# Two softmax attentions on one core: latent attention's scores two steps ahead with logits and maximum in one instruction, selected attention's meta products on 128 rows

## The chip, the core and the metric

The kernel runs on one core of a Trainium2 chip. Five engines work side by side, each through its own queue in order, and meet at semaphores: TensorE (PE; its weight loads are listed as PEld), VectorE (DVE), ScalarE (ACT), GpSimd (POOL) and SyncE (SP), which here only issues transfers. The metric is the device time of one execution, in microseconds (us). The granted clock of TensorE is given as a share of 2.4 GHz: 1.00 is 2.4 GHz, 0.50 is 1.2 GHz.

## What is computed

The reference runs two blocks of two layers each on 512 tokens of width 1024, in float32. Two attentions matter here. The first layer of block one has a selected attention: 8 heads of 64, 16 meta tokens ahead of the 512, and for each query 128 keys chosen by an index score.

```python
_, idx = lax.top_k(score, topk)
kg = take(k, idx)
vg = take(v, idx)
logits = jnp.einsum('bqhd,bqkhd->bhqk', qb, kg).astype(jnp.float32) * dh ** -0.5
bias = rel_bias[rel_bucket(idx - qpos[None, :, None])]
logits = logits + jnp.transpose(bias, (0, 3, 1, 2)).astype(jnp.float32)
p = jax.nn.softmax(logits, axis=-1).astype(v.dtype)
return jnp.einsum('bhqk,bqkhd->bqhd', p, vg)
```

The first layer of block two has a latent attention: 8 heads of 96 for queries and keys and 64 for values, causal.

```python
sc = jnp.einsum('bqhd,bkhd->bhqk', qb, k,
                preferred_element_type=jnp.float32) * scale
sc = jnp.where(kpos[None, :] <= qpos[:, None], sc, -jnp.inf)
p = jax.nn.softmax(sc, axis=-1)
return jnp.einsum('bhqk,bkhd->bqhd', p.astype(v.dtype), v)
```

Everything else is projections, a gated and a retention linear attention, stick-breaking attention, four gated feed-forward layers, pooling and a convolution.

## The kernel before

Nearly all of TensorE's time goes to dense products (`gemm_k`, lines 486, 490, 493), each made of three float32r products of high and low parts. ScalarE makes the high part of the weights (L459), GpSimd the low part (L466).

Both attentions are one class, `Soft`, with three programs that run side by side: `soft_pe`, `soft_dve`, `soft_act`. Queries are taken in tiles of 128 tokens, t = 1 to 4 (selected attention also has t = 0, the 16 meta tokens). A step is one tile and one head, 8 steps per tile, and tile t sees t key tiles of 128 (selected attention: and the 16 meta keys). A step i is made of:

- `scores(i)` on TensorE (L773) into a bank of PSUM;
- `logits(i)` on VectorE: scale and mask or bias into buffer `lg[i % 2]` (L852), then the negated row maximum (L854). It waits until step i-2 has been transposed out of that buffer;
- `exps(i)` on ScalarE (L910): exponential with row sum. It waits for the maximum of i and for the output of step i-2 (`values_out`, L874), since maxima and sums lie in `mx`, two of each;
- `turn(i)` on TensorE: transposes the probabilities, one product per key tile (L788), and one of the 16 meta columns (L785, selected attention only);
- `turned(i)` on ScalarE copies them to `pt` (L919), and VectorE the 16 meta rows (L863, in `spread`); `spread` also has the reciprocal of the row sum (L865);
- `values(i)` on TensorE (L804): probabilities times values, accumulated over the key tiles. The meta keys come first there, with 16 rows of `pt` and `av`;
- `out(i)` on VectorE: times the reciprocal (L874), into `oa` or `moa`. After a tile's last head `mixed` (L818) transposes its outputs, and a copy or gate and a split into high and low follow (L717, L719, L735, L728).

The order is written out by hand. TensorE per step i: scores(i+1), turn(i), values(i-1), then `fill(i)`, dense k-steps of other layers by a table (latent attention: one in each of the first 16 steps, none later; selected attention: one in each of steps 8 to 31, then every other step). VectorE: logits(i+1), evictions of the dense units (`between`), spread(i), out(i-1). ScalarE: exps(i), turned(i-1). GpSimd adds bias and mask for selected attention (`bm`).

`spare` puts products that nobody reads ahead of the scores: in latent attention six per step from step 17 on (L1351), in selected attention six per step from 6 to 23 and in every other step from 33 on (L2417).

## Time and profile before

| | |
|---|---|
| median of 3 runs | 2734.92 us |
| the three runs | 2734.92, 2715.95, 2737.76 us |
| the profiled execution | 2732.96 us |
| its span on the core | 2731.2 us, mean granted clock 0.975 |
| TensorE busy | 2621.8 us, 96% of the span |
| VectorE, ScalarE, GpSimd busy | 1047.4, 881.9, 1075.9 us |
| share of TensorE in the chain that ended last | 88% |
| selected attention | 284 to 470 us of the span |
| latent attention | 1334 to 1420 us of the span |

Busy time of TensorE counts a product from its start to its modelled end, so neighbours overlap, and a busy TensorE is not TensorE at its peak. Float32 products appear as two records each (the trace's counts x4, x8, x10 are such records for scores and values), transpositions and float32r products as one.

### The profile page before, as it was taken

The numbers are of one execution on the slowest core, as the hardware profiler recorded it, in microseconds if no ns is written. First come the engines' busy times: TensorE is split into PE (matmuls) and PEld (weight loads), VectorE is DVE, ScalarE is ACT, GpSimd is POOL, SyncE is SP. The second block draws the span as 40 slices with busy tenths as digits, with TensorE's granted clock in tenths as the row PEclk, the third lists the DMA queues.
The fourth block names the chain that finished last, engine by engine and source line by source line (L and its number), as shares of the span: only waits on it lengthen the run. The fifth ranks groups of instructions, "written<-read, shape, count | busy, mean of one in ns | idle before, by whom it ended". The sixth has DMA issues, their size and how long they took to land.

```text
span 2731.2 us, 32116 instructions
## 1 busy us (share of the span) xinstructions
PE 2621.8 (96%) x13277; PEld 2146.3 (79%) x13277; DVE 1047.4 (38%) x1740; ACT 881.9 (32%) x1289; POOL 1075.9 (39%) x830
## 2 busy tenths in 40 slices
PE   7999899999998999999889999999999999999999
PEld 6888787887566888877677888878888788888887
DVE  3656343424447322255555222252121444421212
ACT  4433322324654222233534222242222322322221
POOL 3223122431114444444205444445444445444443
PEclk9999987998999999999999999999999999999999
DMA  4222000321013233231103233232233232233222
GB/s 127 63 63 84 27 16 16 109 78 47 16 47 103 94 95 105 89 91 49 55 9 108 94 94 106 85 100 93 93 101 99 88 98 93 93 98 100 96 93 77
DMA packets 215852, 217.78 MB, mean 80 GB/s; under 512 B 10600, under 2 KB 213091, under 8 KB 215707
## 3 DMA queue, kind: packets, MB, share of 16 engines
q1 hardware_dynamic: 215504, 215.68, 24.7%
q8 instruction: 105, 1.72, 0.3%
q14 instruction: 41, 0.33, 0.0%
q10 hardware_dynamic: 202, 0.06, 0.0%
HBM read 213.60 MB, written 2.12 MB: 79 GB/s over the span
## 4 chain that ended last, share of the span: by engine, by line
PE 88%; DVE 5%; ACT 3%; issue 2%; POOL 1%; DMA 1%; ACTq 0%; DVEq 0%; SPq 0%
PE ps L490 65%; PE ps L486 8%; PE ps L493 4%; PE ps L804 2%; PE ps L773 2%; POOL wl L466 1%; ACT wh L459 1%; PE ps L788 1%; PE ps L2417 1%; PE ps L2028 1%; PE ps L1992 1%; PE ps L1475 0%; PE ps L1972 0%; DMA raw<-in_w_in_ab 0%; DVE rstd L567 0%
## 5 line engine op out<-in xcount | busy, mean ns | idle before, releaser
L466 POOL TENSOR_TENSOR wl<-raw,wh 128x512 fp32r<-128x512 f32 x794 | 1047.3, 1350 | 1541.9 <-ACT wh L459 1541.9
L490 PE MATMUL ps<-NH,wh 128*128 128x512 f32 (+1 forms) x1824 | 721.0, 395 | 22.0 <-POOL wl L466 11.3
L490 PE MATMUL ps<-NL,wh 128*128 128x512 f32 (+1 forms) x1824 | 715.8, 392 | 0.0
L490 PE MATMUL ps<-NH,wl 128*128 128x512 f32 (+1 forms) x1824 | 715.0, 392 | 0.0
L459 ACT ACTIVATE wh<-raw 128x2048 fp32r<-128x2048 f32 (+4 forms) x219 | 380.6, 1738 | 479.8 <-PE ps L490 429.3
L490 PEld LDWEIGHTS ps<-NH,wh 128*128 128x128 f32 (+1 forms) x1824 | 345.1, 189 | 104.5 <-POOL wl L466 14.4
L490 PEld LDWEIGHTS ps<-NL,wh 128*128 128x128 f32 (+1 forms) x1824 | 344.7, 189 | 74.8 <-issue 1.7
L490 PEld LDWEIGHTS ps<-NH,wl 128*128 128x128 f32 (+1 forms) x1824 | 344.8, 189 | 73.5
L490 PE MATMUL ps<-GH,wl 128*128 128x512 f32 x832 | 332.8, 400 | 0.0
L490 PE MATMUL ps<-GH,wh 128*128 128x512 f32 x832 | 329.8, 396 | 2.3 <-DVE GL L728 2.3
L490 PE MATMUL ps<-GL,wh 128*128 128x512 f32 x832 | 329.6, 396 | 0.0
L986 DVE SCALAR_TENSOR_TENSOR H<-ps,H 128x512 f32<-128x512 f32 x96 | 66.3, 691 | 341.8 <-PE ps L490 341.8
L490 PEld LDWEIGHTS ps<-GL,wh 128*128 128x128 f32 x832 | 157.2, 189 | 39.8
L490 PEld LDWEIGHTS ps<-GH,wh 128*128 128x128 f32 x832 | 157.3, 189 | 39.2 <-issue 2.6
L490 PEld LDWEIGHTS ps<-GH,wl 128*128 128x128 f32 x832 | 157.0, 189 | 36.4
L953 ACT ACTIVATE GH<-tmp 128x512 fp32r<-128x512 f32 x88 | 55.7, 633 | 374.8 <-DVE tmp L979 374.8
L949 ACT ACTIVATE sg<-sg 128x512 f32<-128x512 f32 x88 | 55.6, 633 | 316.8 <-DVE sg L970 316.8
L970 DVE TENSOR_TENSOR sg<-ps,rstd 128x512 f32<-128x512 f32 x66 | 45.6, 691 | 236.8 <-PE ps L490 236.7
L976 DVE TENSOR_TENSOR tmp<-ps,rstd 128x512 f32<-128x512 f32 x66 | 45.6, 692 | 211.9 <-PE ps L490 211.9
L486 PE MATMUL ps<-NH,wh 128*128 128x264 f32 (+1 forms) x448 | 96.4, 297 | 8.6 <-ACT aqT L1599 4.0
L981 DVE TENSOR_TENSOR GL<-tmp,GH 128x512 fp32r<-128x512 f32 x88 | 73.3, 833 | 61.5 <-ACT GH L953 61.5
L493 PE MATMUL ps<-wh,NH 128*128 128x256 f32 (+1 forms) x320 | 91.5, 286 | 2.1 <-ACT bv L1606 2.1
(390 smaller groups left out, 3099.9 us busy)
## 6 DMA issues: line engine op xcount, KB each, us to landing
raw<-in_ffn_w_gate SPq DMA_DIRECT2D x44, 1024.0 KB, 5.4
raw<-in_ffn_w_up SPq DMA_DIRECT2D x44, 1024.0 KB, 5.3
raw<-in_ffn_w_down SPq DMA_DIRECT2D x32, 1024.0 KB, 4.9
raw<-in_w_in_ab SPq DMA_DIRECT2D x16, 1024.0 KB, 5.5
raw<-in_w_in_cd SPq DMA_DIRECT2D x14, 1024.0 KB, 5.0
raw<-in_ffn_w_down SPq DMA_DIRECT2D x16, 768.0 KB, 4.2
raw<-in_c_w_in SPq DMA_DIRECT2D x12, 1024.0 KB, 5.1
raw<-in_w_out_ab SPq DMA_DIRECT2D x8, 512.0 KB, 3.4
```

Of the source, the lines that this page charges most:

```text
L459: nc.scalar.activation(wh[:, b % 2, 0:k, 0:w], raw[:, b % 2, 0:k, 0:w], ACT.Copy).then_inc(S("weights_high"), 1)
L466: ins = nc.gpsimd.tensor_tensor(wl[:, b % 2, ks, 0:w], raw[:, b % 2, ks, 0:w], wh[:, b % 2, ks, 0:w].bitcast(F32), ALU.subtract)
L486: last = nc.tensor.matmul(ps[0:m1 - m0, bank + h, 0:T // 2], w[:, s, k, m0:m1], x(k)[:, h * (T // 2):(h + 1) * (T // 2)], start=start, sto ...
L490: last = nc.tensor.matmul(ps[0:m1 - m0, bank, 0:SEQ], w[:, s, k, m0:m1], x(k), start=start, stop=stop)
L493: last = nc.tensor.matmul(ps[0:n_tok, bank, 0:total], x(k)[:, c0:c0 + n_tok], w[:, s, k, 0:total], start=start, stop=stop)
L773: last = nc.tensor.matmul(ps[0:n, A.score_at[i % len(A.score_at)] + x, 0:w], A.q(h, c0, n), A.k(h, x * w, w), start=True, stop=True)
L804: last = nc.tensor.matmul(ps[0:n, A.value_at[i % len(A.value_at)], 256:256 + HD], A.pt[0:kn, i % 2, a0:a0 + n], A.v(kt, h), start=(x == 0) ...
L949: nc.scalar.activation(sg[:, i, :], sg[:, i, :], ACT.Silu).then_inc(S("gate_silu"), 1)
L953: nc.scalar.activation(GH[:, 2 * p_ + i, :], tmp[:, i, 0:SEQ], ACT.Copy).then_inc(S("hidden_high"), 1)
L970: nc.vector.tensor_tensor(sg[:, i, :], ps[:, bank_of(u + i), :], r, ALU.mult).then_inc(S("evac_dve"), 1)
L981: nc.vector.tensor_tensor(GL[:, 2 * p_ + i, :], tmp[:, i, 0:SEQ], GH[:, 2 * p_ + i, :].bitcast(F32), ALU.subtract).then_inc(S("hidden_low" ...
L986: nc.vector.scalar_tensor_tensor(out=H[:, m, META:T], in0=ps[:, bank_of(u), :], scalar=0.5, in1=H[:, m, META:T], op0=ALU.mult, op1=ALU.add ...
```

## The change

Latent attention (`mla`) gets `ahead=2` and `negated=True`:

- scores(0) and scores(1) are issued first; then per step TensorE runs turn(i), scores(i+2), values(i-1), fill(i), and VectorE between(i), spread(i), logits(i+2), out(i-1);
- logits and row minimum come from one VectorE instruction, `tensor_tensor_reduce`: (scores + mask) times the negated `qroot`, minimum accumulated. The exponential takes them with scale -1. One more instruction negates `qroot` beforehand;
- its spare products are gone.

Both attentions: `mx` has four sums in place of two, and exps(i) waits for the output of step i-4 in place of i-2.

Selected attention (`dsa`) keeps its order and its spare products. The meta product of `values` takes all 128 rows of `pt` and `av` instead of 16; rows 16 to 127 are cleared once (`av` before the selection rounds, `pt` before the attention).

```diff
@@ soft_pe
             for x, kt in enumerate(kts):
-                kn = META if kt == 0 else P
                 a0 = 4 * P if kt == 0 else (kt - 1) * P
-                last = nc.tensor.matmul(ps[0:n, A.value_at[i % len(A.value_at)], 256:256 + HD], A.pt[0:kn, i % 2, a0:a0 + n], A.v(kt, h),
+                last = nc.tensor.matmul(ps[0:n, A.value_at[i % len(A.value_at)], 256:256 + HD], A.pt[:, i % 2, a0:a0 + n], A.v(kt, h),
                                         start=(x == 0), stop=(x == len(kts) - 1))
...
-        scores(0)
+        for i in range(A.ahead):
+            scores(i)
         for i in range(N):
-            if i + 1 < N:
+            if A.ahead == 1 and i + 1 < N:
                 scores(i + 1)
             turn(i)
+            if A.ahead == 2 and i + 2 < N:
+                scores(i + 2)
             if i >= 1:
                 values(i - 1)
@@ soft_dve
+            if A.negated:
+                nc.vector.tensor_tensor_reduce(out=A.lg[0:n, i % 2, 0:w], in0=ps[0:n, s0, 0:w], in1=b, scale=A.scale(t, n, h), scalar=BIG,
+                                               op0=ALU.add, op1=ALU.min, accum_out=A.mx[0:n, i % 2, :]).then_inc(S(tg + "_logits"), 1)
+                return
...
-            step(dve, nc.vector.reciprocal(A.mx[0:n, 2 + i % 2, :], A.mx[0:n, 2 + i % 2, :]))
+            step(dve, nc.vector.reciprocal(A.mx[0:n, 2 + i % 4, :], A.mx[0:n, 2 + i % 4, :]))
...
             spread(i)
+            if A.ahead == 2 and i + 2 < N:
+                logits(i + 2)
             if i >= 1:
                 out(i - 1)
@@ soft_act
-            act.wait_ge(S(tg + "_max"), i + 1)
-            if i >= 2:
-                act.wait_ge(S(tg + "_values_out"), i - 1)
+            act.wait_ge(S(tg + ("_logits" if A.negated else "_max")), i + 1)
+            if i >= 4:
+                act.wait_ge(S(tg + "_values_out"), i - 3)
             w = A.width(t)
-            nc.scalar.activation(A.lg[0:n, i % 2, 0:w], A.lg[0:n, i % 2, 0:w], ACT.Exp, bias=A.mx[0:n, i % 2, :],
-                                 accum_out=A.mx[0:n, 2 + i % 2, :]).then_inc(S(tg + "_exp"), 1)
+            nc.scalar.activation(A.lg[0:n, i % 2, 0:w], A.lg[0:n, i % 2, 0:w], ACT.Exp, bias=A.mx[0:n, i % 2, :], scale=-1.0 if A.negated else 1.0,
+                                 accum_out=A.mx[0:n, 2 + i % 4, :]).then_inc(S(tg + "_exp"), 1)
@@ second_dve
         step(dve, nc.vector.reciprocal(qroot[:, :, :], qroot[:, :, :]))
+        step(dve, nc.vector.tensor_scalar(qroot[:, :, :], qroot[:, :, :], -1.0, None, ALU.mult))
@@ second_pe
-        def mla_spare(i):
-
-            for x in range(MLA_SPARE[i]):
-                nc.tensor.matmul(ps[:, mla.score_at[i % 2], 0:SEQ // 2], GH[:, x % 4, 0:P], GH[:, (x + 1) % 4, 0:SEQ // 2], start=True, stop=True)
-        mla.spare = mla_spare
@@ dsa
-               lambda kt, h: av[0:token_tile(kt)[1], kt, h * HD:(h + 1) * HD],
+               lambda kt, h: av[:, kt, h * HD:(h + 1) * HD],
@@ vector program
         index_dve(dve)
+        nc.vector.memset(av[:, 0, :], 0.0).then_inc(S("av_zero"), 1)
...
+        step(dve, nc.vector.memset(pt[:, :, 4 * P:5 * P], 0.0))
         soft_dve(dve, dsa, lambda e: e.wait_ge(S("strip_out"), HEADS))
```

ScalarE waits for `av_zero` before it writes the first tile of `av`.

TensorE's queue in latent attention at t = 3, in its order. L773 or L775 are scores, L788 or L790 transpositions, L804 or L805 values, L1351 the spare products. Before:

```order
L773 MATMUL ps<-ktT,qtT 128x384
L788 MATMUL ps<-K_53,mlg 128x128 x3
L804 MATMUL ps<-kvtok,mpt 128x64 x3
L1351 MATMUL ps<-GH 128x256 x6
L773 MATMUL ps<-ktT,qtT 128x384
L788 MATMUL ps<-K_53,mlg 128x128 x3
```

and after:

```order
L790 MATMUL ps<-K_53,mlg 128x128 x3
L775 MATMUL ps<-ktT,qtT 128x384
L805 MATMUL ps<-kvtok,mpt 128x64 x3
L790 MATMUL ps<-K_53,mlg 128x128 x3
L775 MATMUL ps<-ktT,qtT 128x384
```

The scores moved from ahead of the transpositions to behind them and belong to a step one later; the six products are gone.

VectorE's queue at the same tile, with a tile's closing copy (L717 or L718) in it: `mlg` are the logits, `mmx` maxima and sums, `moa` the outputs. Before:

```order
L852 SCALAR_TENSOR_TENSOR mlg<-ps,qroot,K_133 128x384
L854 TENSOR_REDUCE mmx<-mlg 128x1
L717 COPY tmp<-ps 128x512
L865 RECIPROCAL mmx<-mmx 128x1
L874 TENSOR_SCALAR moa<-ps,mmx 128x64
```

and after:

```order
L873 RECIPROCAL mmx<-mmx 128x1
L853 ISA mlg,mmx<-ps,K_133,qroot 128x384
L853 ISA mmx 128x1
L882 TENSOR_SCALAR moa<-ps,mmx 128x64
L718 COPY tmp<-ps 128x512
```

The logits of the step after next stand behind the reciprocal and ahead of the output. The one instruction of the source is two rows, the second of which writes one column.

## Rows read from the trace of the kernel before

**Rows 1.** The page, 40 slices of the span, tenths of TensorE's full clock.

```profile
PEclk9999987998999999999999999999999999999999
```

**Rows 2.** Busy time of each engine in four stretches (us from the span's start).

```profile
core 0: us, PE busy (x) PEld busy (x) DVE busy (x) ACT busy (x) POOL busy (x), PEclk, DMA share, GB/s
351.00:380.00 29.00, 28.05 (x195) 23.70 (x194) 14.50 (x45) 8.55 (x26) 9.16 (x10) 1.00 0.06 19
380.00:433.40 53.40, 52.91 (x204) 42.63 (x204) 18.83 (x49) 11.51 (x29) 12.53 (x11) 0.55 0.04 11
1334.00:1367.00 33.00, 27.65 (x146) 20.84 (x147) 20.26 (x66) 14.84 (x51) 4.16 (x4) 1.00 0.11 33
1367.00:1412.40 45.40, 42.82 (x286) 33.48 (x286) 28.30 (x66) 19.63 (x49) 2.51 (x2) 1.00 0.04 12
```

**Rows 3.** Waits in latent attention: engine, line, releaser: total us, times, longest.

```profile
ACT mlg L910 <- DVE moa L874: 39.0, 27, 1.9
PEld ps L788 <- ACT mlg L910: 21.5, 29, 1.7
```

**Rows 4.** Timeline of latent attention, one step at t = 4 (start, duration, instruction).

```profile
1397.54 0.72 ACT L910 ACTIVATE mlg<-mlg,mmx 128x512 f32<-128x512 f32 x1 [1.81 <-DVE moa L874]
...
1397.88 1.02 PE L773 MATMUL ps<-ktT,qtT 96*128 96x512 f32 x2
1398.16 0.19 ACT L910 ACTIVATION_READ_ACCUMULATOR mlg<-mlg,mmx 128x1 f32 x1
...
1398.74 0.60 PE L788 MATMUL ps<-K,mlg 128*128 128x128 f32 x4
...
1399.18 1.00 PE L804 MATMUL ps<-kvtok,mpt 128*128 128x64 f32 x8
...
1399.99 0.96 PE L1351 MATMUL ps<-GH 128*128 128x256 f32 x6
```

**Rows 5.** Waits of TensorE in selected attention, 323 to 470 us.

```profile
PEld ps L804 <- issue: 7.1, 33, 0.6
...
PE ps L486 <- DVE H L1412: 3.3, 6, 1.0
...
PE ps L785 <- ACT lg L910: 1.9, 3, 1.1
```

**Rows 6.** Timeline of TensorE in latent attention, t = 2 and t = 3.

```profile
1359.89 0.44 PE L788 MATMUL ps<-K,mlg 128*128 128x128 f32 x2
...
1361.42 0.59 PE L773 MATMUL ps<-ktT,qtT 96*128 96x256 f32 x2
...
1381.74 0.55 PE L788 MATMUL ps<-K,mlg 128*128 128x128 f32 x3
...
1382.80 0.96 PE L1351 MATMUL ps<-GH 128*128 128x256 f32 x6
```

**Rows 7.** Timeline of VectorE, ahead of latent attention and at t = 4.

```profile
1316.15 0.34 DVE L1246 RECIPROCAL qroot<-qroot 128x32 f32<-128x32 f32 x1
...
1395.58 0.75 DVE L852 SCALAR_TENSOR_TENSOR mlg<-ps,qroot,K 128x512 f32<-128x512 f32 x1 [1.25 <-PE ps L773]
1396.37 0.69 DVE L854 TENSOR_REDUCE mmx<-mlg 128x1 f32<-128x512 f32 x1
```

**Rows 8.** Timeline of TensorE in selected attention, a step at t = 4.

```profile
437.81 0.60 PE L788 MATMUL ps<-K,lg 128*128 128x128 f32 x4
438.34 1.47 PE L804 MATMUL ps<-av,pt 16*128 16x64 f32 x10
```

**Rows 9.** Busy time and granted clock in stretches of 3 us.

```profile
382.00:385.00 3.00, 2.52 (x15) 1.85 (x15) 1.95 (x5) 0.88 (x3) 1.03 (x1) 1.00 0.00 0
385.00:388.00 3.00, 2.99 (x10) 2.41 (x10) 0.40 (x3) 1.10 (x3) 0.00 (x0) 0.52 0.00 0
```

**Rows 10.** Timeline of TensorE before and at the end of the slow stretch.

```profile
382.03 0.94 PE L773 MATMUL ps<-akT,aqT 64*128 64x200 f32 x4
...
385.01 0.67 PE L486 MATMUL ps<-MH,wh 128*128 128x264 f32 x2 [0.49 <-DVE H L1412]
...
430.18 1.52 PE L2417 MATMUL ps<-MH 128*128 128x264 f32 x6
```

More of the change, by code:

```diff
@@ L27 @@
 NEG = -1e30
+BIG = 3e38
 TAKEN = -3e38
@@ L320, in program @@
     bm = at("bm", 17536, [P, 2, T])
-    mx = at("mx", 41832, [P, 4, 1])
+    mx = at("mx", 41832, [P, 8, 1])
     lg = at("lg", 41840, [P, 2, T])
@@ L385, in program @@
     kroot = at("kroot", 24864, [P, NT, HEADS])
-    mmx = at("mmx", 24896, [P, 4, 1])
+    mmx = at("mmx", 24896, [P, 8, 1])
     ropet = at("ropet", 28016, [P, 4, HEADS, ROPE // 2])
@@ L740, in __init__ @@
         def __init__(self, tag, tiles, q, k, v, width, scale, bias, off, lg, pt, oa, mx, gate, tile0, meta, banks, fill=None, between=None,
-                     oa_first=None, gate_ready=None, spare=None, one_bank=False):
+                     oa_first=None, gate_ready=None, spare=None, one_bank=False, ahead=1, negated=False):
             self.tag, self.tiles, self.q, self.k, self.v = tag, tiles, q, k, v
@@ L747, in __init__ @@
             self.oa_first, self.gate_ready, self.spare, self.one_bank = oa_first, gate_ready, spare, one_bank
+            self.ahead, self.negated = ahead, negated
             self.own_mix = self.mix_at not in self.score_at and self.mix_at != self.meta_at
@@ L874, in out @@
             nc.vector.tensor_scalar(A.rows_of(ti)[0:n, h * HD:(h + 1) * HD], ps[0:n, A.value_at[i % len(A.value_at)], 256:256 + HD],
-                                    A.mx[0:n, 2 + i % 2, :], None, ALU.mult).then_inc(S(tg + "_values_out"), 1)
-        logits(0)
+                                    A.mx[0:n, 2 + i % 4, :], None, ALU.mult).then_inc(S(tg + "_values_out"), 1)
+        for i in range(A.ahead):
+            logits(i)
         for i in range(N):
-            if i + 1 < N:
+            if A.ahead == 1 and i + 1 < N:
                 logits(i + 1)
@@ L1009, in program @@
     MLA_KSTEPS = [1] * 16 + [0] * 16
-    MLA_SPARE = [0] * 17 + [6] * 15
     MLA_ENDS = [3, 7, 11, 15]
@@ L1029, in program @@
                lambda dve, i, t, h, n, w: const("causal", SEQ - P * t, w), META, mlg, mpt, moa, mmx, None, 4, False, ((0, 1), (4, 6), None, (5,), 7),
-               None, mla_between, one_bank=True)
+               None, mla_between, one_bank=True, negated=True, ahead=2)
     def second_sp(sp):
@@ L1604, in ab_act @@
             act.wait_ge(S("parts_ready"), 1)
+            if name == "av" and i == 0:
+                act.wait_ge(S("av_zero"), 1)
             dst = {"av": av, "bv": bv}[name][0:n, i, (b - FIRST[name]) * BC:(b - FIRST[name] + 1) * BC]
```

## The prediction

> **What bounds the kernel now.** I read the page first: TensorE is busy almost throughout, and at its full granted clock in nearly every slice; the exceptions to look at are the sixth and the seventh slice of 68 us, 341 to 478 us [rows 1]. So a change pays only where TensorE waits, issues what nobody needs, or is granted 1.2 instead of 2.4 GHz. The two attentions are those places; I read their stretches next [rows 2]. Both run 8 heads per tile of 128 queries, one "step" per head, and a tile t has t key tiles.
>
> Latent attention takes 78.4 us (1334.0 to 1412.4), 33.0 for t = 1 and 2, 45.4 for t = 3 and 4, at a granted clock of 1.00 throughout. What ends last in a step: ScalarE starts the exponential only when the output of two heads earlier has left PSUM (39.0 us in 27 waits), and TensorE then waits for that exponential before it can transpose the probabilities (21.5 us on its weight loads) [rows 3]. One step of t = 4 shows it [rows 4]: scores end at 1398.90, though their exponential belongs to the next step; the exponential that the transpositions at 1398.74 needed had started only at 1397.54, after 1.81 us of waiting for the output copy. TensorE fills part of that with six products that nobody reads (L1351, 1399.99 to 1400.79, 0.80 us).
>
> Selected attention is another case. TensorE waits little there: 1.9 us for exponentials, 3.3 us for an evicted bank [rows 5]. But from 385 to 433 us it works at 1.2 GHz: 53.4 us at a mean of 0.55 for nine steps, against 29.0 us for the eight steps before, at 1.00 [rows 2].
>
> **The change, part by part.** Times are of the profiled execution, 2732.96 us (span 2731.2), which is 2 us under the median of the three shown.
>
> 1. Latent attention, order. The logits of step i+2 are now made before the output of step i-1, and the exponential of step i needs only the output of four steps earlier. So exp(i+1) runs while TensorE transposes step i. What then sets the pace? TensorE's own issue, from rows without a wait. t = 4 [rows 4]: transpositions and values 1.25 us (1398.74 to 1399.99), scores of 512 columns 0.86 (1397.88 to 1398.74): 2.11. t = 3 [rows 6]: 1.06 (1381.74 to 1382.80) and three quarters of 0.86: 1.71. t = 2, with a dense k-step inside: 1.53 (1359.89 to 1361.42) [rows 6] and half of 0.86: 1.96. t = 1 is t = 2 less one transposition (0.11), two value records (0.22) and a quarter of 0.86 (0.21): 1.42. Eight of each make 57.6; three closings of a tile, four transpositions each, 1.2; 0.05 us of change-over per step, my allowance, 1.6; a first exponential to wait for, 1.1, and 0.8 before the first logits: 62.3. Against 78.4 that is **16.1 us less**. This already holds the removed products: they are simply not in the sums.
>
> 2. Does another engine take over? VectorE is busy for 28.3 us in the 16 steps of t = 3 and 4, 1.77 each, ScalarE 19.6, 1.23 each [rows 2], against the 1.91 that TensorE would need on average. Of VectorE's share at t = 4 the logits take 0.75 and the maximum 0.69 [rows 7]. The new instruction is one pass plus a second row that reads the accumulator (the order shows two). No row shows it. Lower bound 0.75, as the logits alone; upper 1.44, as both; I take 0.75 + 0.19, the 0.19 being ScalarE's read of its accumulator [rows 4]. Even at the upper bound VectorE needs no more than now, 1.77 of 1.91, so the value hardly matters for the sum; it returns as a rival. The loop over the two logit buffers: transpositions 0.44, scores 1.02, logits 0.94, exponential and its read 0.81, about 3.3 us per two steps, under 4.2. At the end of the attention the last maximum is no longer on the path: **0.6 us less** [rows 7].
>
> 3. One more VectorE instruction negates qroot, behind the reciprocal at 1316.15 [rows 7]. TensorE waits for the keys behind it, so nothing hides it; between nothing (it overlaps ScalarE's root) and the reciprocal's 0.34 on the same 32 columns, I take **0.2 us more**. Clearing av once (128x512) and the meta columns of pt: the VectorE of that time is in its selection rounds, and between its last one and the first logits it idles for some 3 us, so both hide; if not, about 0.8 us. I book **0.3 us more**.
>
> 4. Meta products on 128 rows. 32 steps have a 16-row meta product between 128-row work. Four transpositions and ten value records run from 437.81 to 439.81, 2.00 us [rows 8]; the latent attention's four and eight from 1398.74 to 1400.18, 1.44, plus 0.22 for two more records, 1.66 [rows 4]. So a 16-row product costs 0.3 us beside its own time, and the trace books 7.1 us in 33 waits as issue before these loads [rows 5]. I take the row count itself as free. In a quarter of the steps the dense work that follows waits for a bank that VectorE has yet to free (six waits [rows 5]), and there the time only becomes wait. 12 of 16 steps of t = 1, 2 and 6 of 8 of t = 4 gain 0.3: 5.4. Those of t = 3 gain 0.3 to 0.35: 2.0. The later limit on the exponential gives back the 1.9 us of waits [rows 5]. Together **9.3 us less**.
> The Trainium skill's page TensorEngine Tiling, Key Properties, says that changing the tiling mode drains TensorE; the rows above agree and give it a price here. By that page alone there would be no figure, and the sum is the same.
>
> 5. The clock of t = 3. Behind the scores at 382.03 no spare products stand any more, and the next dense product waited for its bank until 385.01 [rows 10]; in that moment the grant fell to 0.5 [rows 9]. It stayed there until 433 (5 us at 1.00 and 48 at 0.50 make the 0.55 of [rows 2]), after dense and spare products had come together again at 430.18 [rows 10]. The eight steps at full clock would be those of t = 2 (3.63 us each) less 0.80 of spare products, plus some 0.5 of more keys: 3.3, and one of t = 4 at 4.3, 31 us instead of 53.4: the fall costs 22 us. One of the three times shown, 2715.95, is 19 and 22 us under the others, which is what a run without this fall would be; I read it so, without a profile to show it. The fall is thus a near thing. The change makes TensorE's array do eight times as many rows in each meta product, in the very stretch before the fall, and takes the 16-row drain out; the hole until 385.01 stays, as it hangs on scores, VectorE's logits and the eviction behind them. I expect the clock to hold more often than not: **22 us less**.
>
> Sum: 2732.96 - 16.1 - 0.6 + 0.2 + 0.3 - 9.3 - 22 = 2685.5; I say 2686.
>
> **Rivals.**
> A. The clock falls at 385 as before. For it: the hole before 385.01 is untouched [rows 10], and three profiles or times of four seem to have it. Then 2686 + 22 = 2708.
> B. The handover still sets latent attention's pace: the new instruction is slow, or logits wait for reciprocal and eviction in VectorE's queue. Its point is 2.11 us per t = 4 step; at 2.4 instead, and 0.3 more in the others, 32 x 0.3 = 10 us are not gained: 2696. Against it: VectorE is busy only 28.3 of 45.4 us now [rows 2].
> C. The other side: with the unread products gone, TensorE loses its clock in latent attention, and nothing there brings it back. For it: they were 0.80 us of each of the last 15 steps [rows 4]. Against it: in their place comes work without waits, 2.1 us of every 2.1. If the grant fell at the start of t = 2, the sums of step 1 would double: 8 x (1.96 + 1.71 + 2.11) x 2 = 92 instead of 46, so 46 us more. With A it is 2754; with the clock of t = 3 kept, 2732. It decides as soon as one early fall meets no recovery.
> The Trainium skill's page TensorE: Matmul & The Clock Gate, Part 4, says that a transposition does not count as TensorE being busy in the same way. By that page C is likelier, as t = 3 and 4 are then left with scores and values only; no row here shows it, and 1372 to 1412 stays at 1.00 with them plus the spare products.
> D. No effect of the 128 rows beyond the clock: 2695 with the clock kept.
>
> **Chances.** Forecast (with small misses inside) 0.48, A 0.32, B 0.07, C 0.08, D 0.05. The range takes the forecast, A, B and D with 5 us on either side for allowances: 2674 to 2714; its own range for the likeliest case is 2674 to 2697. A measurement of this kernel can tell about 1% from no change. 1% below 2734.92 is 2707.6: the forecast, B and D are under it, A about on it (a third of it counts as faster), C mostly within or above: faster 0.70, same 0.26, slower 0.04.
>
> **What would show it.** Right: ScalarE's waits for moa gone, TensorE's waits for mlg under 5 us, no L1351, latent attention 62 to 64 us long, t = 3 at about 14 to 15 us; in selected attention no issue wait before the values, x10 values in about 1.2 us. The clock row of 380 to 433 decides between the forecast and A. Wrong: an accumulator instruction above 1.4 us; a grant of 0.5 between 1340 and 1412; TensorE waiting for logits instead of exponentials.

## The result and the profile after

The changed kernel takes 2677.3 us (median of 6 runs, 2674.4 to 2680.5), the kernel before, timed beside it, 2723.6 (6 runs, 2710.9 to 2737.8): a ratio of 0.985, with a 95% interval of 0.9815 to 0.9881. The forecast was 2686. The profiled execution took 2674.43, its span is 2672.6.

The median of before is a mixture. Over all its 65 runs there are two kinds: 42 at 2706.6 to 2719.3 us (median 2711.4, mean granted clock 0.981 to 0.987 where it is listed, for 59 of the 65) and 23 at 2731.3 to 2743.4 (median 2736.4, clock 0.971 to 0.976), and nothing between. The 25 us between them are put down to the fall of the clock in selected attention's third tile, t = 3, for which the profiles give 21 (below). Each kernel has one profiled execution; for its other runs a fall is read from time and mean clock alone. The profile of before is of the second kind, so against it the change brings 58.5 us, against a run without the fall 34.

The page's clock row of after, against [rows 1]; then the stretches of the attentions, against [rows 2], whose columns it has: stretches that nearly are selected attention's tiles with one, two and three key tiles, the first 27 us of the tile with four, and two halves of latent attention up to the next dense product:

```profile
PEclk9999999999999999999999999999999999999999
```

```profile
323.00:349.00 26.00, 24.01 (x184) 21.45 (x184) 11.23 (x44) 6.80 (x27) 8.22 (x12) 1.00 0.14 42
349.00:376.00 27.00, 25.32 (x194) 22.86 (x193) 14.56 (x44) 8.54 (x26) 9.19 (x10) 1.00 0.07 20
376.00:403.00 27.00, 24.86 (x178) 21.37 (x178) 16.87 (x45) 10.25 (x26) 11.30 (x10) 1.00 0.06 20
403.00:430.00 27.00, 25.66 (x180) 21.65 (x179) 16.45 (x38) 9.59 (x22) 7.87 (x6) 1.00 0.01 2
1299.70:1331.00 31.30, 29.64 (x177) 24.46 (x178) 17.58 (x79) 19.36 (x60) 6.10 (x6) 1.00 0.11 35
1331.00:1364.10 33.10, 29.33 (x195) 23.11 (x194) 17.58 (x62) 17.72 (x43) 0.26 (x1) 0.95 0.05 17
```

The third tile of selected attention (376 to 403) runs at 1.00 where before had 0.55. Latent attention has 1.00 up to its closing; the 0.95 is a fall of 6.8 us that begins at 1360.8, behind the start of the last values (1360.07). Before had one there too, 10.2 us from 1416.0.

Where the time went, by the start of a tile's first scores to that of the next tile's, and for the last tile to the next dense product behind the attention (us):

| stretch | before | after | |
|---|---|---|---|
| start to selected attention | 284.1 | 285.5 | +1.4 |
| selected attention, t = 0 | 38.6 | 37.0 | -1.6 |
| t = 1, 2 | 27.4, 28.9 | 25.7, 26.9 | -3.7 |
| t = 3 | 44.8 | 26.6 | -18.2 |
| t = 4 | 46.8 | 38.2 | -8.6 |
| between the attentions | 863.7 | 859.7 | -4.0 |
| latent attention, t = 1 to 3 | 13.2, 18.7, 22.5 | 9.5, 14.4, 15.3 | -15.3 |
| t = 4 with closing | 33.7 | 25.3 | -8.5 |
| rest | 1308.7 | 1308.5 | -0.2 |

Selected attention gives 32 us, latent attention 24. The rows at the top and between the attentions hold no edit that could save or cost so much. They go with short falls of the clock: the grant is 0.5 for 3.4 to 10.2 us at a time, in places that differ from execution to execution. Between the attentions these add up to 50.9 us before and 43.4 after; half of the difference, what work at half clock would cost, is 3.8 of the 4.0. Ahead of selected attention they are 13.6 and 17.0 us, half of the difference 1.7 for the +1.4. The 1.6 of t = 0 are of this kind as well: before had 3.4 us at 0.5 from 286.1 in it, after had none.

The waits of latent attention after (engine, line, releaser: total us, times, longest), against [rows 3]:

```profile
ACT mlg L921 <- DVE mmx L853: 13.0, 20, 1.0
PEld ps L805 <- issue: 5.0, 19, 0.6
PEld ps L790 <- ACT mlg L921: 3.0, 4, 1.3
```

ScalarE's 39.0 us for the output are gone; it waits 13.0 for the minimum, most of which TensorE does not feel. TensorE's 21.5 us for exponentials are 3.0, in 4 waits instead of 29. Two steps of t = 4 on TensorE, against [rows 4]:

```profile
1351.12 0.61 PE L790 MATMUL ps<-K,mlg 128*128 128x128 f32 x4
1351.57 1.02 PE L775 MATMUL ps<-ktT,qtT 96*128 96x512 f32 x2
1352.43 1.00 PE L805 MATMUL ps<-kvtok,mpt 128*128 128x64 f32 x8
1353.27 0.61 PE L790 MATMUL ps<-K,mlg 128*128 128x128 f32 x4
```

Transpositions 0.45, scores 0.86, values 0.84: 2.15 us from one transposition to the next, with no wait. The chain of work that ended last goes through TensorE alone here; its shares by line from 1340 to 1356:

```profile
by line: PE ps L775 37.7%; PE ps L805 37.4%; PE ps L790 22.8%; PE ps L819 2.8%; issue 0.1%
```

The same step on VectorE, the new instruction against [rows 7]:

```profile
1352.72 0.75 DVE L853 CUSTOM_DVE_ANT_0 mlg<-ps,K,qroot 128x512 f32<-128x512 f32 x1 [1.05 <-PE ps L775]
1353.40 0.08 DVE L853 DVE_READ_ACCUMULATOR2_ANT mmx<- 128x1 f32 x1
1353.47 0.28 DVE L882 TENSOR_SCALAR moa<-ps,mmx 128x64 f32<-128x64 f32 x1
1353.67 0.15 DVE L873 RECIPROCAL mmx<-mmx 128x1 f32<-128x1 f32 x1
```

The two records of logits and minimum, 0.75 and 0.08 us, overlap: 0.76 from the start of the one to the end of the other, where logits and maximum took 1.48 (1395.58 to 1397.06) [rows 7]. VectorE idles 1.05 us of the step.

### The profile page after: what moved, and what is told of

Same layout as the page of the kernel before. It is cut to its first block, busy times and chain, and to the rows that moved or that the text cites. A ratio compares the mean times of both kernels' runs of the same rounds, so it can differ in the third digit from the quotient of the medians.

```text
span 2672.6 us, 31908 instructions
## 1 busy us (share of the span) xinstructions
PE 2569.0 (96%) x13187; PEld 2114.8 (79%) x13187; DVE 1032.1 (39%) x1743; ACT 881.8 (33%) x1289; POOL 1075.1 (40%) x830
## 4 chain that ended last, share of the span: by engine, by line
PE 87%; DVE 6%; ACT 3%; issue 2%; POOL 1%; DMA 1%; ACTq 0%; DVEq 0%; SPq 0%
PE ps L491 66%; PE ps L487 8%; PE ps L494 3%; PE ps L775 2%; PE ps L805 1%; POOL wl L467 1%; ACT wh L460 1%; PE ps L790 1%; PE ps L2000 1%; DVE score L1585 1%; PE ps L2427 1%; PE ps L1980 1%; DVE top L1584 1%; PE ps L2036 0%; PE ps L1481 0%
## 5 line engine op out<-in xcount | busy, mean ns | idle before, releaser
L491 PEld LDWEIGHTS ps<-NH,wh 128*128 128x128 f32 (+1 forms) x1824 | 344.6, 189 | 107.3 <-POOL wl L467 18.2
L997 DVE SCALAR_TENSOR_TENSOR H<-ps,H 128x512 f32<-128x512 f32 x96 | 66.3, 691 | 341.9 <-PE ps L491 341.9
```

What stands on the lines that cost most here:

```text
L491: last = nc.tensor.matmul(ps[0:m1 - m0, bank, 0:SEQ], w[:, s, k, m0:m1], x(k), start=start, stop=stop)
L997: nc.vector.scalar_tensor_tensor(out=H[:, m, META:T], in0=ps[:, bank_of(u), :], scalar=0.5, in1=H[:, m, META:T], op0=ALU.mult, op1=ALU.add ...
```

## Experiments

Twelve kernels. "Changed" is the kernel after, "before" the one before. Spans of the attentions are as in the table above. Latent attention's includes its closing.

### Latent attention: which part brings what

**Four sums alone**, in the kernel before:

```diff
-            if i >= 2:
-                act.wait_ge(S(tg + "_values_out"), i - 1)
+            if i >= 4:
+                act.wait_ge(S(tg + "_values_out"), i - 3)
```

> The kernel before with one part of the change alone: four sums in place of two, and the exponential waits for the output of four steps earlier. Theory: ScalarE's waits for the output go, TensorE's waits for the exponential of latent attention (8.9 us on its products) go for the larger part, and the first to the last scores of latent attention take 70 us instead of 77; nothing in selected attention but the 2 us of waits. Rival, that the order is what matters and this alone only turns the wait for the output into one for the maximum: 76 us or more. The clock in selected attention's third tile as in before, fallen in some runs.

Measured: 10 runs, median 2716.8, 2700 to 2732: five at 2700 to 2705, five at 2728 to 2732, with the clock's fall in selected attention. The unfallen ones (median 2701.4) are 10 us under those of before. Latent attention takes 82.5 us for 88.2, and in it TensorE still waits for exponentials:

```profile
ACT mlg L910 <- DVE mmx L854: 32.4, 25, 2.5
...
PEld ps L788 <- ACT mlg L910: 11.9, 20, 1.4
```

The theory holds. From the first to the last scores it is 71.7 us where 70 were expected and before had 76.8, and this execution had a fall of 3.4 us in tile t = 1 (from 1308.6) that before's did not have. It costs some 1.4: the tile took 12.8 us, and 11.4 without a fall in the next kernel, whose program is the same there. So the four sums bring some 7.1 us at full clock.

**Four sums and no unread products**, in the kernel before (the same edit, and the `mla.spare` line gone):

> The kernel before with four sums in place of two, and without latent attention's 15 x 6 unread products. With four sums alone latent attention takes 82.5 us to the next dense product. Theory: the unread products are work on TensorE's path as soon as the exponential comes early, so taking them out gives up to 15 x 0.80 = 12 us, less what turns into waiting for the exponential, since with scores one step ahead 2.1 us of TensorE's work stand against 1.44 for logits and maximum, 0.9 for the exponential and its read, and hand-overs: some 0.5 us per step at three and four key tiles. Latent attention 74 to 78 us, at a clock of 1.00 to its last tile. Rival, that these products hold the clock: 0.5 within the third or fourth tile, 85 us or more.

Measured: 10 runs, median 2707.0, 2693.8 to 2726.5, three with the full fall in selected attention and two near 2712. Latent attention 73.6 us, 8.9 less than with four sums alone, at 1.00 up to its closing. Just under the expected 74. Of the 8.9, 1.4 are the fall in t = 1 just named; the products themselves bring 7.5 (t = 3 and 4, 17.1 and 28.6 us for 20.8 and 32.4). Of their 12 us, 4.5 turned into waits; those of TensorE's loads for the exponential grew from 11.9 to 18.0 us, its products' from 4.6 to 7.3:

```profile
PEld ps L788 <- ACT mlg L910: 18.0, 23, 2.2
PE ps L788 <- ACT mlg L910: 7.3, 10, 1.4
```

**One instruction, scores one step ahead**, in the changed kernel:

```diff
-               None, mla_between, one_bank=True, negated=True, ahead=2)
+               None, mla_between, one_bank=True, negated=True)
```

> The changed kernel with latent attention's scores one step ahead, as before (the one instruction, the four sums and no unread products stay). Between the end of scores and the transpositions of the same step TensorE then has 2.1 us of other work at four key tiles and 1.6 at three; the chain beside it is 0.83 for logits with minimum, 0.9 (0.75 at three) for the exponential and its read, and hand-overs of some 0.3. Theory: they are about equal, so two steps ahead is worth little once the other parts are there: 1 to 4 us, latent attention 65 to 68 us instead of 64.4. Rival, the order is the main part of the gain: 72 us or more.

Measured: 2684.1 (4 runs, 2680.0 to 2685.5), latent attention 66.9 us. The theory holds: the order alone is worth 2.5 us of it once the rest is there. TensorE's weight loads wait 9.8 us for exponentials, for 18.0 in the kernel above and 3.0 in the changed one. The medians differ by 6.8, more than that; the runs scatter by 5.

**Two instructions, scores two steps ahead**, in the changed kernel (`negated=True` and the negation of `qroot` out):

> The changed kernel with logits and maximum of latent attention as two vector instructions again, and no negation of qroot. Theory: TensorE sets the pace; VectorE then needs some 2.0 us of every 2.15 at four key tiles and 1.6 of every 1.6 at three, so it costs 0 to 5 us in all and the one instruction is not what brought the gain: 2677 to 2682. Rival, the one instruction is needed for it: VectorE or the loop over the two logit buffers becomes the bound, 0.3 us or more per step, 2687 or more.

Measured: 2680.1 (4 runs, 2677.1 to 2682.9), latent attention 67.8 us, of which some 1.5 is a fall of the clock for 3.4 us that this execution had in its first tile (from 1301.2; the changed program's first tile takes 9.5 us without such a fall and 11.0 with it, in the two kernels further down that have 16 rows or the unread products). The time is where the theory had it. Its tiles 3 and 4 take 15.8 and 26.1 us for 15.3 and 25.3. So the one instruction is worth 1.3 us there, against a forecast of 0 to 5 in all. TensorE's loads wait 3.6 us for exponentials.

The four together make a table of latent attention without unread products: 73.6 with neither, 66.9 with the instruction, 67.8 with the order (some 66.3 without its fall), 64.4 with both. Each is one execution. Each of the two nearly suffices, as each takes much of the wait for the exponential off TensorE's path (18.0 us of its loads' waits become 9.8 and 3.6): the one by a shorter chain, the other by more work beside it. The terms don't add.

**The unread products back**, in the changed kernel:

> The changed kernel with latent attention's unread products back (six per step from step 17 on, 0.80 us each step). Theory: TensorE sets the pace, so each of the 15 is on its path: 12 us more, 2689, latent attention 76 us instead of 64.4; the clock was not held by them. Rival: part of them falls into waits that the trace of the changed kernel does not show, or they shorten the fall of the clock behind the last tile: 5 to 9 us more.

Measured: 2684.7 (4 runs, 2684.4 to 2690.2), latent attention 74.6 us. A step of t = 4 there:

```profile
1358.11 0.97 PE L1363 MATMUL ps<-GH 128*128 128x256 f32 x6
1358.91 1.02 PE L775 MATMUL ps<-ktT,qtT 96*128 96x512 f32 x2
1359.78 1.00 PE L805 MATMUL ps<-kvtok,mpt 128*128 128x64 f32 x8
1360.61 0.61 PE L790 MATMUL ps<-K,mlg 128*128 128x128 f32 x4
1360.97 0.95 PE L1363 MATMUL ps<-GH 128*128 128x256 f32 x6
```

2.86 us from one group of them to the next for 2.15, so 0.71 a step, not 0.80, and tiles 3 and 4 take 19.6 and 29.6 us, 8.6 more in all. Of the 10.2 by which the whole is longer, the rest is a fall of 3.4 us in the first tile. The theory's 12 was too high: the 8.6, and the 7.4 between the medians, lie in the rival's 5 to 9. The fall at the closing is as long as without them, 6.8 us; no run shows that they held a clock.

### Selected attention: rows, breaks and the clock

**16 rows again**, in the changed kernel:

```diff
+                kn = META if kt == 0 else P
-                ... A.pt[:, i % 2, a0:a0 + n] ...
+                ... A.pt[0:kn, i % 2, a0:a0 + n] ...
```

> The changed kernel with one thing undone: the meta product of values takes 16 rows again (the rows are still cleared). Theory: 16-row products between 128-row work cost 0.3 us each beside their own time, so with the clock kept it is about 9 us slower than the changed kernel's 2677, 2686; and since the array then does less in the stretch before the third tile, the granted clock of that tile falls to 0.5 again in at least half of the runs, 22 us each: a median of 2686 to 2708 and a mean clock near 0.977 in the runs that fall. Rival, the clock at that place has nothing to do with the rows (it only goes by where the hole ahead of it happens to fall): the clock is kept in nearly all runs, as in the changed kernel, and the time is 2684 to 2688.

Measured: 2684.0 (4 runs, 2683.9 to 2688.3), no fall in any of the four. Tiles 1 to 4 take 27.4, 28.8, 28.3 and 40.4 us, together 124.9. With 128 rows they take 117.4 (25.7, 26.9, 26.6, 38.2, in the kernel with latent attention's unread products and in the changed one alike). So the rows are worth 7.5 us at full clock, as forecast (5.4 + 2.0). The expectation's 9 counted the waits for the exponential in, which this kernel keeps saved. Two steps on TensorE, with 16 rows and, behind, in the changed kernel:

```profile
376.11 0.28 PE L787 MATMUL ps<-K,lg 128*16 128x128 f32 x1
376.22 0.38 PE L790 MATMUL ps<-K,lg 128*128 128x128 f32 x2
376.53 1.02 PE L806 MATMUL ps<-av,pt 16*128 16x64 f32 x6
377.36 0.49 PE L487 MATMUL ps<-MH,wh 128*128 128x264 f32 x2
```

```profile
373.33 0.28 PE L787 MATMUL ps<-K,lg 128*16 128x128 f32 x1
373.44 0.38 PE L790 MATMUL ps<-K,lg 128*128 128x128 f32 x2
373.66 0.78 PE L805 MATMUL ps<-av,pt 128*128 128x64 f32 x6
374.25 0.49 PE L487 MATMUL ps<-MH,wh 128*128 128x264 f32 x2
```

From the meta transposition to the dense product 1.25 us and 0.92: 0.33 a step, for 16 rows of the array in place of 128: the smaller product is the dearer one. The Trainium skill's page TensorEngine Tiling (Array Packing), Key Properties, says that a change of the tiling mode drains TensorE; the two steps agree, if a 16-row product among 128-row ones is such a change, and put 0.33 us on it.

On the clock this run decides nothing. The times are the rival's (2684 to 2688, no fall), but the two kernels with the same selected attention fell in 8 of 20 runs, and at that rate four in a row without a fall come in one case of eight.

**128 rows alone**, in the kernel before:

> The kernel before with one part of the change alone: meta products on 128 rows (with both clearings). Theory: no run falls in the third tile of selected attention, mean clock 0.983 or more in each, and the time is 31 us under that of a run of before with the fall, 9 us under one without: 2701. Rival, rows do nothing for the clock: about half of the runs fall, so 2701 in some and 2723 in others.

Measured: 2705.5, 10 runs, 2702.3 to 2707.2, mean clock 0.983 to 0.986 in each. No fall, where the kernel before fell in 5 of 19 runs on the same chip. What the theory says of the clock holds, though 10 runs alone are thin for it (at 5 of 19, ten without a fall come in one case of twenty). The time is 6 us under an unfallen run of before, where 9 were forecast, and 31 under a fallen one.

**An unread product beside the 16 rows**, in the kernel before:

```diff
+                if kt == 0 and t:
+                    nc.tensor.matmul(ps[0:n, A.value_at[i % len(A.value_at)], 384:384 + HD], A.pt[:, i % 2, 0:n], A.v(1, h), start=True, stop=True)
```

> The kernel before, with its 16-row meta products, and in each step from the second tile on one product more that nobody reads, of 128 rows and 64 columns (probabilities times the first key tile's values, into unused columns of the bank), ahead of the meta product. It does for the array's work what 128 rows do, and leaves the 16-row products where they are. So far about a third of the runs with 16-row products fell to 0.5 in the third tile (13 of 39), and none of 20 with 128 rows. Theory, the array's work keeps the clock: no run falls, all at about 2711 + 3 = 2714. Rival, it is the break that a 16-row product makes between 128-row products: about a third of the runs fall, near 2736.

Measured: 12 runs, 2712.8 to 2723.1, mean clock 0.982 to 0.987; none fell in the third tile, where the kernel before beside it fell in 11 of 23. The place at which before fell, with [rows 2]'s columns, and the dense product behind the hole:

```profile
388.00:391.00 3.00, 2.80 (x19) 2.15 (x17) 1.78 (x4) 0.98 (x3) 1.03 (x1) 1.00 0.00 0
```

```profile
391.19 0.48 PE L486 MATMUL ps<-MH,wh 128*128 128x264 f32 x2 [0.38 <-DVE H L1414]
```

With the breaks of the 16-row products all in place the clock held, so it can hold without taking them out; a product of 128 rows more per step was enough. The busy time of TensorE does not tell the kernels apart: of the 3 us that end at that dense product it is busy for 2.51 before and 2.45 in the kernel with four sums and no unread products of latent attention, which both fell, and for 2.45 also with four sums alone, which held in its profile; it is busy for 2.62 here, and for 2.17 and 2.11 with 128 rows (alone and in the changed kernel), which held. What the edits share is more 128-row products of the array in each step; that they also move the hole in time, this one later and the 128 rows earlier in the tile, is not ruled out as the cause. Its price was more than forecast, 2718 for 2714: tiles 1 to 3 take 28.3, 29.9 and 29.6 us, 0.9 to 1.3 more than with 16 rows at full clock, and this execution has a later fall (17.1 us from 450.5) of its own, at the end of t = 4.

Over all batches, before fell in 23 of 65 runs, the two kernels with its rows and four sums in 8 of 20 (two others half), the one with 16 rows in the changed kernel in 0 of 4. With 128 rows, or the unread product, and the unread products of selected attention as they were: 0 of 40. The rate of before differs from batch to batch (below), and four of the 40 stand beside a batch in which before did not fall either. What the fall looks like in a kernel with 16 rows (four sums, no unread products in latent attention), stretches by [rows 2]'s columns:

```profile
386.00:389.00 3.00, 2.64 (x17) 1.89 (x15) 1.77 (x4) 0.97 (x4) 1.03 (x1) 1.00 0.00 0
389.00:392.00 3.00, 2.81 (x10) 2.37 (x10) 0.59 (x4) 0.57 (x3) 0.00 (x0) 0.57 0.00 0
392.00:450.00 58.00, 58.00 (x212) 46.84 (x212) 19.37 (x49) 11.98 (x29) 13.07 (x11) 0.50 0.03 10
```

and what the changed kernel does at the very same place:

```profile
379.16 0.78 PE L805 MATMUL ps<-av,pt 128*128 128x64 f32 x6
380.83 0.48 PE L487 MATMUL ps<-MH,wh 128*128 128x264 f32 x2 [0.89 <-DVE H L1418]
```

The hole is still there, and its wait is longer than before's (0.89 for the 0.49 of [rows 10]); the grant stays at 1.00. The second stretch shown begins 0.4 us ahead of the fall (389.4), which lasted 61.4 us.

### Towards a better kernel

**Selected attention's unread products out too**, in the changed kernel:

```diff
-    DSA_SPARE = [0] * 6 + [6] * 18 + [0] * 8 + [0, 6] * 4
+    DSA_SPARE = [0] * 40
```

> The changed kernel without selected attention's unread products as well (18 steps of six, and four of six in the last tile, 0.8 us each: 17.6). Theory: with 128 rows the array has enough to do and the clock is kept: 8 to 17 us less than the changed kernel, 2660 to 2669, as part of the time turns into waits for banks and exponentials. Rival, the clock falls in the first or second tile and stays down to the fourth: 30 to 70 us more, 2705 to 2745.

Measured: 2664.3 (4 runs, 2660.7 to 2665.0), ratio to before 0.977 (0.972 to 0.983), in the middle of the forecast; no run fell. Tiles 1 and 2 take 20.7 and 22.5 us for 25.7 and 26.9, t = 4 35.2 for 38.2.

**Unread products in the closing holes**, on top of that (`hold` issues so many products of 256 or 264 columns):

```diff
+        A.hold(4)
         values(N - 1)
+        A.hold(3)
         mixed(len(A.tiles) - 1)
+        A.hold(14)
```

> The changed kernel without selected attention's unread products (2664 us in the run before), and with unread products in the closing holes of both attentions instead: 4 ahead of the last values, 3 ahead of the last transposition of outputs, 14 behind it, while VectorE and ScalarE copy and split. In the runs so far the clock fell to 0.5 in these holes for 3.4 to 6.8 us in each attention, so 1.7 to 3.4 us of dense work is lost in each. Theory: TensorE's own work in the holes keeps the grant at 1.00, 2 to 6 us less in all: 2658 to 2662. Rival: the products run at half clock themselves and delay the dense work behind them, or the fall comes later; no gain, 2662 to 2668.

Measured: 2671.7 (4 runs, 2670.7 to 2677.1), mean clock 0.980 to 0.982: slower by 7, outside theory and rival. The closings gained what was forecast, though not where the expectation below of the kernel with both looks for it. The last tile of each attention takes as long as without the added products (35.2 and 24.8 us to the next dense product; the 33.4 and 23.0 told there end among the 14 unread products). Without them and with them, last values, next dense product and the one behind it:

```profile
419.31 1.30 PE L805 MATMUL ps<-av,pt 128*128 128x64 f32 x10 [0.54 <-DVE oa L882]
...
423.91 0.78 PE L487 MATMUL ps<-MH,wh 128*128 128x264 f32 x2 [2.26 <-DVE ML L729]
424.48 0.64 PE L487 MATMUL ps<-ML,wh 128*128 128x264 f32 x2
```

```profile
435.39 1.30 PE L805 MATMUL ps<-av,pt 128*128 128x64 f32 x10
...
439.99 0.48 PE L487 MATMUL ps<-MH,wh 128*128 128x264 f32 x2 [0.55 <-DVE ML L729]
440.30 0.41 PE L487 MATMUL ps<-ML,wh 128*128 128x264 f32 x2
```

4.60 us in both. What is gained is the dense work behind, which runs at 1.00 instead of 0.50 for 5.0 and 5.6 us (the 6.8 us at 0.5 from 422.1 and from 1353.9 are gone), by estimate half of that each, 5.3 us in all. But in the profiled run the clock fell in the tile t = 1 (the second, counting t = 0), far ahead of the added products, for 37.5 us:

```profile
320.00:326.00 6.00, 4.07 (x30) 3.26 (x31) 2.96 (x11) 2.46 (x8) 3.19 (x4) 1.00 0.26 87
326.00:329.00 3.00, 3.00 (x18) 2.60 (x17) 1.03 (x6) 0.67 (x3) 0.49 (x1) 0.61 0.00 0
329.00:362.00 33.00, 32.49 (x138) 28.83 (x138) 12.12 (x45) 7.08 (x26) 7.73 (x10) 0.50 0.05 17
```

TensorE was busy for 4.07 of the 6 us ahead of it: this is where t = 1 starts and TensorE waits for exponentials and banks. The tiles t = 1 and 2 take 30.3 and 28.0 us for 20.7 and 22.5: the fall costs 15. So the 2664 of the kernel above stands on four runs in which that place held; these four (all with a clock that low) stand on four in which it did not. It ran on another chip; whether chip or layout decided it is open.

**Scores two steps ahead in selected attention**, without the closing products (`ahead=2` for `dsa`, no unread products):

> The changed kernel without selected attention's unread products (2664 us), with selected attention's scores two steps ahead as well, its logits and maximum still two instructions. TensorE's waits for its exponential there are 3.5 us in 5 and 5.2 us on loads. Theory: they go, 3 to 5 us less, 2659 to 2661. Rival: VectorE's logits and maximum (1.47 us at four key tiles) now stand between the reciprocal and the output and ahead of nothing that TensorE needs sooner, while the evictions of the dense units come no earlier: the waits for banks (5.8 us) stay or grow, and the time is 2664 to 2672.

Measured: 2655.2 (4 runs, 2649.7 to 2659.0), ratio 0.9795 (0.9774 to 0.9815). More than expected: tiles 0 to 3 take 32.2, 20.3, 20.2 and 24.6 us for 36.4, 20.7, 22.5 and 26.6. The last tile takes 0.5 more. TensorE's waits for an evicted bank (5.8 us in 7) are gone as well, likely since the dense unit's products now lie behind more work of the attention itself. A stretch of t = 2, t = 3 and the start of t = 4:

```profile
335.00:390.00 55.00, 55.00 (x391) 47.23 (x391) 37.70 (x104) 23.25 (x61) 24.99 (x24) 1.00 0.10 30
```

TensorE without a gap, and at 1.00, with no unread product in selected attention.

**Both**:

> The two better versions together: the changed kernel without selected attention's unread products, its scores two steps ahead there too (2655 us), and the 4, 3 and 14 unread products in the closing holes of both attentions. In the run with those products alone the last tile's time fell by 1.8 us in selected and by 1.8 us in latent attention (33.4 for 35.2, 23.0 for 24.8), while a fall of 37.5 us that began in selected attention's second tile, ahead of any of them, cost some 15 us. Theory: the two add up, 2651 to 2652, if the clock holds in the second tile as it did with scores two steps ahead (4 of 4 runs). Rival: the fall of the second tile comes back in some or all of the runs, since nothing unread stands there: 2663 to 2668, mean clock 0.982 or less.

Measured: 2650.3 (6 runs, 2649.1 to 2652.1), ratio 0.974 (0.970 to 0.978), mean clock 0.988 to 0.989 in each run. The theory holds. This is the best kernel of the study, 27 us under the changed one. Its two attentions and their clocks (selected, then latent), each ending among the 14 unread products of its closing (the next dense products come at 414.98 and 1340.91); neither closing has a fall, and one of 3.4 us at the start of each makes the 0.99 and 0.97:

```profile
282.00:413.10 131.10, 126.98 (x936) 111.13 (x937) 70.71 (x221) 53.12 (x131) 43.67 (x44) 0.99 0.07 21
1275.50:1339.10 63.60, 61.33 (x381) 50.01 (x382) 34.19 (x139) 36.45 (x102) 6.38 (x6) 0.97 0.08 26
```

## Why the prediction was right, and where not

**The sum.** From the profile before to the profile after 47.5 us were forecast and 58.5 measured. Of the 11 between them, 7.1 are latent attention, 0.7 selected attention (31.3 forecast, 32.0 measured) and 3.3 the rest of the kernel, where 0.5 more was forecast for the extra instructions and 2.8 less was measured, which goes with the short falls there. Against an unfallen run of before the change brings 34, and the parts measured one by one give 33: 23.8 in latent attention, 7.5 for the rows, 1.9 for the later limit.

**Latent attention's bound.** Right: TensorE's own issue sets the pace, and the waits it named are gone. The size was off: forecast 16.1 + 0.6 us less, measured 23.8. The step that failed is the comparison. 62.3 us for all 32 steps were set against 78.4 that ended at 1412.4, while before's last values start at 1416.79 and end at 1418.73: the stretch cut a step and a half off before, but not off the sum. From the first scores to the end of the last values before took 84.4 us (from 1334.30) and after takes 60.7 (1299.70 to 1360.35). So 6.0 of the miss is the wrong end, and the sum for the new kernel was 1.6 too long. That 1.6 is small because errors cancel: steps of t = 1 to 4 take 1.25, 1.81, 1.60 and 2.14 us, not 1.42, 1.96, 1.71 and 2.11, so eight of each 54.4 for 57.6, and the change-over of 0.05 a step (1.6) is not there; against these 4.8 stand some 3 us at the ends of the attention that the sum lacks. The sign "62 to 64 us long" was met by 64.4 only because the closing is in the 64.4 and not in the sum: that was luck. The part that no error touches, up to the values of step 29, is 77.7 before (1334.3 to 1412.00) and 56.3 after (1299.7 to 1356.04), 21.4 less; the end behind it, 10.5 and 8.0 us to the next dense product, gives the other 2.5, where 0.6 was forecast, and part of that is that before's clock was down for the last 6.5 us of it and after's for 3.3.

**The new instruction.** 0.76 us at 512 columns, its two overlapping records (0.75 and 0.08) together, where 0.94 was taken between 0.75 and 1.44. The sum did not hang on it, as said; the runs put 1.3 us on it in tiles 3 and 4 with scores two ahead (some 1.9 in all), and 6.7 with scores one ahead (73.6 to 66.9).

**The extra instructions.** The negation took 0.18 us behind the reciprocal, as booked. The clearing of pt (0.27 us, at 282.41) lies in 3 us of idle time, that of av (0.49 us, at 121.36) far ahead of the attention; the 0.3 booked is not seen.

**Meta products.** Forecast 7.4 for the rows and 1.9 for the later limit. Measured 7.5, and 1.9 for the limit (selected attention with 128 rows alone 158.0 us, in the changed kernel with latent attention's unread products back 156.1). The issue wait before the values, 7.1 us in [rows 5], is 0.8 after; TensorE's waits for the bank grew from 3.3 to 5.8, as the prediction said of a part of the steps.

**The clock of the third tile.** Forecast 22 us for the fall, measured 21: selected attention's 32.0, less 7.5 for the rows, 1.9 for the limit and 1.6 for the short fall in t = 0. (The tiles alone, 44.8 for 28.3 and 46.8 for 40.4 with 16 rows, give 22.9, with the limit's share counted in.) That the change keeps the clock had a chance of 0.60 (the forecast, B and D together); it does in every run. Of the two reasons given, the missing break was not needed: the unread product kept the clock with the breaks in place. More array work in the stretch before fits all runs that kept selected attention's unread products, but a shift of the hole in time was not tested apart from it, so the cause of the clock's holding is narrowed down and not shown. What was wrong is how often before falls: "three of four" was read from four numbers, and it is 23 of 65. A forecast of the median of before from three runs was a draw from two kinds.

**The rivals.** A, the clock falls anyway: not in any of 40 runs. B, the hand-over still sets the pace: no, 3.0 us of waits. C, the clock is lost in latent attention: in the changed kernel's profile the grant is 1.00 through transpositions, scores and values until the closing. In the profiles of five of the kernels that share its latent attention or add to it (16 rows, unread products back, the kernel without selected attention's, and the two with scores two steps ahead in both) it fell in the first tile, but came back after 3.4 us; "nothing there brings it back" is wrong, and such a fall costs 1.5 us, not 46. The Trainium skill's page TensorE: Matmul & The Clock Gate, Part 4, says that a transposition does not count as busy in the same way; the trace does not contradict it, since a step has 0.45 us of transpositions beside 1.70 of scores and values, but it decided nothing here. D, no effect of the rows beyond the clock: no, 7.5 us.

## What to carry to other kernels

Ask of each stretch which wait ends last there, and shorten the chain or put more work beside it; when two edits both take the same wait away, the second brings much less than alone (here 2.5 us for some 7.3 and some 1.9 for 6.7). When a stretch with its own sum is compared with the trace, let both end at the same instruction. And where runs of a kernel differ by 1% in two groups, look for a fall of the clock and count it over many runs, before a change is credited with a median. In single profiles, take out the short falls of each before their stretches are compared.

## What the runs showed of the hardware

- Where its neighbours have 128 rows, a matrix product of 16 rows costs a third of a microsecond more than one of 128 in its place (1.25 for 0.92 us from the meta transposition to the dense product).
- The clock fell with TensorE busy: 2.64 of 3 us ahead of the fall in a kernel with 16 rows, 2.52 of 3 in the kernel before [rows 9]. With one product of 128 rows more in each step, and otherwise the same program, it held at that place in 12 of 12 runs, by their times and mean clocks, and with 128 rows in the meta products behind a longer hole (0.89 us) too, with TensorE busy for 2.11 of the 3 us up to its end.
- Once down, it stayed down for 48 us (before) and 61 us (four sums, no unread products in latent attention), in the latter with the engine busy for every microsecond (58.00 of 58.00). The fall of 48 us costs 21; that of 61 us some 27 (t = 3 and 4 take 44.7 and 50.6 us, 28.3 and 40.4 with four sums alone and no fall). Elsewhere falls of 3.4 us end by themselves, as in latent attention's first tile, and cost 1.5.
- The same program falls in some executions and not in others: 23 of 65, but 11 of 23 in one batch and none of 7 in another.
- Logits with an accumulated minimum (0.75 us at 512 columns) cost VectorE the same as logits alone (0.75); the read of the accumulator (0.08) lies but for 0.01 us within it. ScalarE's read of its accumulator takes 0.19.
